# One decoder step with a 32-expert layer: products that nobody reads ahead of the first gather, the first extra job written out, and the memory key weights in two loads

## What is computed

```python
def memory_kv(mem, g_mem_kv, w_mk, w_mv):          # 256 memory tokens
    m = rmsnorm(mem, g_mem_kv)
    k = (m @ w_mk).reshape(b, n, MEM_HEADS, MEM_HD)
    v = (m @ w_mv).reshape(b, n, MEM_HEADS, MEM_HD)

def moe_ffn(h, ...):                                # 32 experts, 4 for each token
    logits = (xt @ w_router) + b_router
    top_val, top_idx = lax.top_k(logits, TOP_K)
    gates = jax.nn.softmax(top_val, axis=-1)
    ...
        g = jnp.minimum(xblk @ w_gate[e] + b_gate[e], 7.0)
        u = jnp.clip(xblk @ w_up[e] + b_up[e], -7.0, 7.0)
        a = (u + 1.0) * (g * jax.nn.sigmoid(1.702 * g))
        return a @ w_down[e] + b_down[e]            # times the gate, added to the token

y_prompt, y_sample = rmsnorm(x, g_final)
```

## Time and profile before

| what | value |
|---|---|
| median of 3 runs | 1349.05 us (1343.01 to 1349.41) |
| the profiled execution, its own time | 1347.15 us |
| its span in the trace | 1345.3 us |
| TensorE busy | 1291.2 us (96%) |
| VectorE busy | 450.1 us (33%) |
| moved by DMA | 463.37 MB, 344 GB/s over the span |
| mean granted clock | 0.982 |

### The profile page before, as it was taken

One profiled execution on the slowest core, in us unless ns is written; L12 is line 12 of the kernel. 1 busy time (PEld: TensorE's weight loads), 2 busy tenths in 40 slices (PEclk: granted clock), 3 DMA queues, 4 the chain that ended last, 5 costly groups with the idle time before them and its releaser, 6 DMA issues.

```text
span 1345.3 us, 15553 instructions
## 1 busy us (share of the span) xinstructions
PE 1291.2 (96%) x6088; PEld 523.6 (39%) x6088; DVE 450.1 (33%) x1124; ACT 217.1 (16%) x442; POOL 15.5 (1%) x20
## 2 busy tenths in 40 slices
PE   7999898999799999999999999999999999999996
PEld 3665654556433333333333333333333333333332
DVE  1168778334532222322223322223222222222233
ACT  3014433314311010101001011101111101010102
POOL 0100020000000000000000000000000000000000
PEclk9999899999789999999999999999999999999998
DMA  9701132490879999999999999999999999999993
GB/s 343 280 12 42 36 111 94 169 393 1 340 307 411 426 428 427 428 429 428 429 427 427 428 427 428 428 428 429 427 428 428 427 428 428 428 429 427 427 427 120
DMA packets 44265, 463.37 MB, mean 344 GB/s; under 512 B 5206, under 2 KB 6166, under 8 KB 17860
## 3 DMA queue, kind: packets, MB, share of 16 engines
q1 hardware_dynamic: 42700, 453.54, 80.6%
q0 software_dynamic: 1536, 9.44, 1.9%
HBM read 460.04 MB, written 3.28 MB: 344 GB/s over the span
## 4 chain that ended last, share of the span: by engine, by line
PE 79%; DMA 14%; DVE 5%; ACT 1%; issue 1%; SPq 0%; ACTq 0%; DVEq 0%
PE psum L891 42%; DMA ring<-in_w_up 13%; PE psum L866 6%; PE psum L324 6%; PE psum L907 4%; PE psum L403 3%; PE psum L884 2%; PE psum L363 2%; PE psum L619 2%; DVE ring L1543 1%; PE psum L742 1%; PE psum L381 1%; PE psum L911 1%; PE psum L590 1%; PE psum L748 1%; DMA ring<-in_w_mk 1%
## 5 line engine op out<-in xcount | busy, mean ns | idle before, releaser
L891 PE MATMUL psum<-ring,work 128*64 128x512 f32 x3168 | 702.1, 597 | 7.3 <-DMA ring<-in_w_up 7.3
L891 PEld LDWEIGHTS psum<-ring,work 128*64 128x64 f32 x3168 | 221.5, 137 | 478.2 <-issue 446.6
L1927 DVE TENSOR_SCALAR work<-psum 128x512 f32<-128x512 f32 x32 | 22.1, 692 | 378.9 <-PE psum L891 378.9
L866 PE MATMUL psum<-H,work 128*64 128x512 f32 (+1 forms) x408 | 101.0, 614 | 1.4 <-DVE work L1818 1.4
L1936 DVE TENSOR_SCALAR work<-psum 128x512 f32<-128x512 f32 x32 | 22.1, 692 | 170.1 <-PE psum L891 170.1
L1891 DVE TENSOR_TENSOR X<-X,psum 128x512 f32<-128x512 f32 x68 | 46.7, 686 | 90.0 <-PE psum L907 89.9
L1543 DVE SCALAR_TENSOR_TENSOR ring<-ring,cwT 128x256 f32<-128x256 f32 x240 | 72.5, 377 | 0.1
L1408 ACT COPY work<-psum 128x512 f32<-128x512 f32 x32 | 18.7, 586 | 292.7 <-PE psum L866 292.7
L1415 ACT COPY work<-psum 64x512 f32<-64x512 f32 x32 | 18.5, 578 | 286.6 <-PE psum L891 286.6
L324 PE MATMUL psum<-C,work 128*128 128x128 f32 (+5 forms) x371 | 57.1, 288 | 6.6 <-DMA work<-in_small_rows 6.4
L324 PEld LDWEIGHTS psum<-C,work 128*128 128x128 f32 (+5 forms) x371 | 49.0, 187 | 31.1 <-issue 22.4
(11 more groups left out here) (291 smaller groups left out, 913.3 us busy)
## 6 DMA issues: line engine op xcount, KB each, us to landing
ring<-in_w_gate SPq DMA_DIRECT2D x66, 2048.0 KB, 24.3
ring<-in_w_up SPq DMA_DIRECT2D x66, 2048.0 KB, 25.9
ring<-in_w_down SPq DMA_DIRECT2D x66, 2048.0 KB, 27.9
ring<-in_w_in SPq DMA_DIRECT2D x1, 4096.0 KB, 27.3
ring<-in_cache_mem_k SPq DMA_DIRECT2D x8, 512.0 KB, 14.8
ring<-in_cache_mem_v SPq DMA_DIRECT2D x8, 512.0 KB, 16.3
ring<-in_w_in SPq DMA_DIRECT2D x1, 2688.0 KB, 22.3
ring<-in_w_mk SPq DMA_DIRECT2D x1, 2048.0 KB, 10.3
```

The costliest lines, as they stand in the source:

```text
L866: last = mm(psum[64 * nh:64 * nh + 64, 2, :], Ph[0:ROWS[tt], tt, :], xn[0:ROWS[tt], tt, 512 * nh:512 * nh + 512], start=tt == 0, stop=tt == 2)
L891: last = mm(psum[64 * nh:64 * nh + 64, bank, :], src[:, j, 64 * half:64 * half + 64], w[:, half, j, 512 * nh:512 * nh + 512], start=first ...
```

## The change

1. Start: `small_rows` is issued ahead of `mem`, and `wmk` comes in two loads of 1 MB with a semaphore each. PE does inner blocks 0 to 3 for both memory tiles, then 4 to 7.
2. Router: `keep_warm` issues products of the identity with itself into a PSUM bank that nobody reads, 10 ahead of the wait for `routed`, 5 ahead of the wait for `p_built`.
3. The first extra job is no longer the first round of a loop but written out for all engines, and done whether there is one or not (where there is none, its ranks are moved away by 1000, so that nothing is selected). Its gate and up products stand between the five pieces of the last pair. The gather of a job to come is gone; a loop for jobs 2 and on gathers for itself at its beginning.
4. ACT squares and takes the root of each tile as soon as its x is final (`ov_scm`), into ring slot 3, not after all three.

```diff
+            emptied(pe, V, ("mT", 1, 1))
+            pe.wait_ge(s.load_wmk, 16)
+            keys = [A.open(pe, ("mk", tt)) for tt in range(2)]
+            for k0 in (0, 4):
+                if k0:
+                    pe.wait_ge(s.load_wmk2, 16)
+                for tt in range(2):
+                    for k in range(k0, k0 + 4):
+                        last = mm(keys[tt], mT[:, k, 128 * tt:128 * tt + 128], wmk[:, k, :], start=k == 0, stop=k == KD - 1)
+                    if k0:
+                        last.then_inc(s.full_a, 1)
...
+            def keep_warm(n):
+                for _ in range(n):
+                    mm(psum[:, 1, 0:128], ident, ident, start=True, stop=True)
+            keep_warm(10)
             pe.wait_ge(s.routed, 1)
...
             last.then_inc(s.rank_full, 1)
+            keep_warm(5)
...
+            pe.wait_ge(s.ov_xtm, 1)
+            pe.wait_ge(s.ov_p, 1)
+            biases(0)
+            for half in range(2):
+                pe.wait_ge(ring_in[0][half], (1 + USES) * 16)
+                product(0, XT[0], 0, half, False, half == 1).then_inc(ring_used[0][half], 1)
+            turn_gates(s.ov_pt)
             pe.wait_ge(s.y_moved, NE + 1)
             pe.wait_ge(s.pgt_moved, NE // 2 + 1)
-            for piece in range(5):
-                scatter_pair(piece, NE // 2 + 1, 5 * (NE // 2))
+            scatter_pair(0, *last_pair)
+            scatter_pair(1, *last_pair)
+            for half in range(2):
+                pe.wait_ge(ring_in[1][half], (1 + USES) * 16)
+                product(1, XT[0], 1, half, False, half == 1).then_inc(ring_used[1][half], 1)
+            scatter_pair(2, *last_pair)
+            scatter_pair(3, *last_pair)
+            pe.wait_ge(s.ov_a, 1)
+            turn(4, AA, s.ov_at)
+            scatter_pair(4, *last_pair)
+            pe.wait_ge(s.ov_atm, 1)
+            for half in range(2):
+                pe.wait_ge(ring_in[2][half], (1 + USES) * 16)
+                product(2, AT, 2, half, half == 0, half == 1).then_inc(ring_used[2][half], 1)
+            pe.wait_ge(s.ov_ym, 1)
+            pe.wait_ge(s.ov_ptm, 1)
+            pe.wait_ge(s.sc_free, 5 * (NE // 2) + 7)
+            for tt, bank in enumerate(OV_BANKS):
+                for nh in range(2):
+                    last = scatter_one(tt, nh, 0, bank)
+                last.then_inc(s.ov_sc, 1)
...
-                    pe.wait_ge(s.ov_p, n + 1)
-                    gather(s.ov_xg)
...
             dma(C[:, 0:128], a["constants"][:, 0:128]).then_inc(s.load_ident, 16)
+            dma(small_rows, a["small_rows"]).then_inc(s.load_ident, 16)
             dma(mem, a["mem_prompt"][0].rearrange("(t p) d -> p t d", p=P)).then_inc(s.load_mem, 16)
-            dma(small_rows, a["small_rows"]).then_inc(s.load_ident, 16)
-            dma(wmk, rows_of(a["w_mk"][0])).then_inc(s.load_wmk, 16)
+            dma(wmk[:, 0:4, :], rows_of(a["w_mk"][0])[:, 0:4, :]).then_inc(s.load_wmk, 16)
+            dma(wmk[:, 4:8, :], rows_of(a["w_mk"][0])[:, 4:8, :]).then_inc(s.load_wmk2, 16)
...
+            job = sp.value_load(jobs[0:1, 1:2], min_val=0, max_val=NE - 1)
+            for kind in range(3):
+                src = weights(kind, job)
+                for half in range(2):
+                    sp.wait_ge(ring_used[kind][half], USES)
+                    load_half(kind, half, src)
...
+            f(small[:, 17:18], eps[:, :], ACT.Sqrt)
+            for tt in range(3):
+                act.wait_ge(s.ov_scm, tt + 1)
+                last_root(tt)
...
+            gate_of(1)
+            dve.wait_ge(s.sc_free, last_pair[1] + 2)
+            add_scattered(0, *last_pair)
+            add_scattered(1, *last_pair)
+            up_of(1)
+            add_scattered(2, *last_pair)
+            turned_of(1)
+            add_scattered(3, *last_pair)
+            add_scattered(4, *last_pair)
+            dve.wait_ge(s.sc_free, last_pair[1] + 7)
+            further = dve.value_load(jobs[0:1, 0:1], min_val=0, max_val=JOBS)
+            add_of(1)
```

More of the change, by code:

```diff
@@ L121 @@
+            self.place_full, self.spread_ready, self.lists_full, self.ov_rank, self.load_ident, self.load_lat,
+            self.qz_ready, self.load_wmk2, self.load_wout2, self.load_wout3, self.full_s, self.free_s, self.part_full,
+            self.part_moved, self.gates_ready, self.gt_full,
+        ) = [new(f"signal{i}") for i in range(109)]
 class Lane:
@@ L1418, in _, with last_root @@
             further = act.value_load(jobs[0:1, 0:1], min_val=0, max_val=JOBS)
-            with act.If(further > 0):
-                with act.Fori(1, further + 1) as n:
+            act.wait_ge(s.ov_gc, 1)
+            f(sgm, gm, ACT.Sigmoid, scale=ALPHA).then_inc(s.ov_sg, 1)
+            act.wait_ge(s.ov_pt, 1)
+            nc.scalar.copy(PgT[0], psum[:, 5, 0:T]).then_inc(s.ov_ptm, 1)
+            act.wait_ge(ring_used[2][1], 1 + USES)
+            nc.scalar.copy(Y[0][0], psum[:, 2, :]).then_inc(s.ov_ym, 1)
+            def last_root(tt):
+                r = ROWS[tt]
+                n = st(f(squares[0:r, tt, :], X[0:r, tt, :], ACT.Square, accum_out=small[0:r, 8 + tt:9 + tt]))
+                st.wait(n)
+                f(small[0:r, 11 + tt:12 + tt], small[0:r, 8 + tt:9 + tt], ACT.Sqrt, bias=eps[0:r, :],
+                  scale=1.0 / D).then_inc(s.x_root, 1)
+            f(small[:, 17:18], eps[:, :], ACT.Sqrt)
+            for tt in range(3):
+                act.wait_ge(s.ov_scm, tt + 1)
+                last_root(tt)
+            with act.If(further > 1):
+                with act.Fori(2, further + 1) as n:
+                    act.wait_ge(s.ov_xg, n - 1)
+                    nc.scalar.copy(XG, psum[:, 2, :]).then_inc(s.ov_xgm, 1)
                     act.wait_ge(s.ov_gc, n)
@@ L1424, in _ @@
                     nc.scalar.copy(PgT[0], psum[:, 5, 0:T]).then_inc(s.ov_ptm, 1)
-                    act.wait_ge(s.ov_xg, n)
-                    nc.scalar.copy(XG, psum[:, 2, :]).then_inc(s.ov_xgm, 1)
                     act.wait_ge(ring_used[2][1], n + USES)
                     nc.scalar.copy(Y[0][0], psum[:, 2, :]).then_inc(s.ov_ym, 1)
-            f(small[:, 17:18], eps[:, :], ACT.Sqrt)
-            act.wait_ge(s.x_done, 1)
-            for tt in range(3):
-                r = ROWS[tt]
-                n = st(f(xn[0:r, tt, :], X[0:r, tt, :], ACT.Square, accum_out=small[0:r, 8 + tt:9 + tt]))
-                st.wait(n)
-                f(small[0:r, 11 + tt:12 + tt], small[0:r, 8 + tt:9 + tt], ACT.Sqrt, bias=eps[0:r, :],
-                  scale=1.0 / D).then_inc(s.x_root, 1)
+                act.wait_ge(s.x_done, 1)
+                for tt in range(3):
+                    last_root(tt)
         @block.vector
@@ L1910, in _ @@
             first = dve.value_load(jobs[0:1, 1:2], min_val=0, max_val=NE - 1)
+            base = lists[:, NE + 1:NE + 2]
+            st(v.tensor_scalar(place[:, 2:3], base, 0.0, -1000.0, ALU.is_equal, ALU.mult))
+            st.wait()
             for tt in range(3):
                 r = ROWS[tt]
[L1913 to L1914 removed]
+                v.tensor_scalar(routing[0:r, tt, 2, NE:NE + 1], routing[0:r, tt, 2, bass.ds(first, 1)], base[0:r],
+                                place[0:r, 2:3], ALU.subtract, ALU.subtract)
                 v.tensor_copy(routing[0:r, tt, 1, NE:NE + 1], routing[0:r, tt, 1, bass.ds(first, 1)])
@@ L1952, in _ @@
             dve.sem_inc(s.ov_xtm, 1)
-            last = 5 * (NE // 2)
-            dve.wait_ge(s.sc_free, last + 2)
-            for piece in range(5):
-                add_scattered(piece, NE // 2 + 1, last)
-            dve.wait_ge(s.sc_free, last + 7)
-            further = dve.value_load(jobs[0:1, 0:1], min_val=0, max_val=JOBS)
-            with dve.If(further > 0):
-                with dve.Fori(1, further + 1) as n:
-                    take_job(n + 1)
-                    dve.wait_ge(ring_used[0][1], n + USES)
-                    v.tensor_scalar(gm, psum[:, 0, :], LIMIT, None, ALU.min).then_inc(s.ov_gc, 1)
-                    dve.wait_ge(s.ov_rank, n + 1)
-                    dve.wait_ge(s.ov_pt, n)
+            last_pair = NE // 2 + 1, 5 * (NE // 2)
```

115 lines of the change are left out of this document (61 added, 54 removed).

## The result

The changed kernel takes 1331.47 us (median of 4 runs, 1329.55 to 1332.83) against 1346.24 us for the kernel before on the same chip (median of 4, 1343.01 to 1349.41). The ratio is 0.9889, interval 0.9856 to 0.9923: 1.1% faster. The forecast was 1331, with 1325 to 1341 as its range. The profiled execution took 1331.66 us; its span is 1329.5 us and its mean granted clock 0.992.

The account below looks back on a forecast made before the run. The prediction took the stream of expert weights, full from the third refill on, to bound the kernel. Start 1.9, router 7.6, extra job 5.1 and final norm 1.8 sum to 16.4 us: 1347.15 to 1330.8, said as 1331, range 1325 to 1341.

Parts of the forecast that it names:

- What bounds the kernel: Expert stage: the weight stream runs without stop from the third refill, so a microsecond earlier at expert 0's gate counts fully.
- the ceiling that the forecast worked out: Router: the gain cannot exceed the hole in the weight stream by much; at most 8.2 us.
- Start, 1.9 us: Key products: `mT` rather than 2 MB of key weights ends the wait, at 10.6 instead of 12.54; gain 1.9 us.
- Router, 7.6 us: Logits to expert 0's gate product: unread products bring the clock back before the gather; gain 7.6 us.
- gather 2.72 instead of 5.61 [...] gate 9.69 to 7.02: Router: gather and expert 0's gate product at full clock, worth 3.15 and 2.67 us.
- The price of 0.5 us for an unread product: Router: a 128x128 product costs 0.5 us at 1.2 GHz and 0.25 at 2.4 GHz, read from L859.
- Extra job, 5.1 us: Expert 31's end to the job's down product: 33.7 us shrink to 28.6 without useless gather, turnings and waits; gain 5.1 us.
- without that cover 2.3 us would be open: Extra job: pieces 2 to 4 cover DVE's two operations up to `AA` (1.6 us) and the `AT` copy (0.7 us).
- Final norm, 1.8 us: End of kernel: ACT's squares start after the first addition, DVE's scalings follow its additions; gain 1.8 us, 1.0 to 2.2.
- The clock that doesn't come back: Rival at the router: clock still low before the gather, which runs at 1.2 GHz; 1340 (to 1342) us; chance 0.13.
- The clock that falls again: Rival between gather and first gate product: clock returns, then falls; some 3.5 of 7.6 us missing, 1334.5 us; chance 0.15.
- The slower case: Rival: useless products in the way, clock at 1.2 GHz far into the expert loop; 1356 us with one expert; chance 0.03.

Follow-up runs that it names:

- e_piecesfirst_fill: Changed kernel with the last pair's five pieces ahead of all the job's products, plus six unread products behind the up product; 1336.69 us, ratio 0.9937.
- e_same: The kernel before, unchanged, run again; 1344.58 us (median of 12), ratio 0.9998.
- e_warm: The kernel before with only the 10 and 5 unread products added; 1341.30 us (median of 12), ratio 0.997.
- e_nowarm: The changed kernel without its 15 unread products; 1336.17 us (6 runs), ratio 0.9926.
- e_rootlate: The changed kernel with ACT's squares and roots begun only after DVE's third addition; 1335.28 us (6 runs), ratio 0.9929.
- e_piecesfirst: Changed kernel with the last pair's five pieces put back ahead of the job's products; useless gather and loop stay out; 1336.45 us, ratio 0.9938.
- e_nostart: The changed kernel with the old order of loads and old loop of key products; 1333.12 us (6 runs), ratio 0.9918.
- e_warm10_0: The changed kernel with the first 10 unread products but without the 5 ahead of the gather; 1335.48 us (5 runs), ratio 0.9914.
- e_fill: The changed kernel with 4, 2 and 1 more unread products in the waits ahead of the router's logits; 1331.37 us (5 runs), ratio 0.9907.

## Why the prediction was right

The time was hit (1331 for 1331.47), and of each of the four parts some gain is there in the profiles. The sizes of the terms came out less well, and part of the hit is luck, as shown below. By term, against the pair of profiles:

*What bounds the kernel.* Right. Behind the third refill the stream is full from about 398 on (thirteenth slice, 428), ends 9.7 us earlier, and the end moved with it and with the tail. Of the 9.4 us by which the third refill was issued earlier, 8.4 arrived at the last wait for weights. What became of the other 1.0 us isn't shown. It needn't be the ceiling that the forecast worked out: in e_piecesfirst_fill the gate product ends 1.7 us earlier still (374.71) and the landing comes 2.4 us earlier (1269.61), with nothing lost.

*Start, 1.9 us.* Half of it. `mT` does end the wait, but the key products begin at 11.58, not at 10.6: `mem` landed at 7.07 and its turning could not begin earlier, so all of it hangs on a transfer that I had moved by 0.3 us only. They end 0.8 us earlier in this pair. Over four profiles with the old start and nine with the new one the ends are 1.7 us apart in the mean, but they overlap (40.28 to 44.05 and 38.72 to 41.81), and the times say 1.1, within their noise. (The forecast put 0.43 us against 29.43 / 64, which is 0.46; it bears on nothing.)

*Router, 7.6 us.* Right for the execution it was read from, too large for the kernel. Logits to gate product shrank from 27.9 to 20.1 us, 7.8, as the sum had it: ten products in 3.94 us (forecast below 4.4), gather 2.97, gate 7.02, clock back at about 360, where about 361.7 was forecast. But the same program has 22.1 us in e_same, and the two comparisons by time give 3 to 4 us (e_warm) and 2.2 to 4.1 (e_nowarm). The step that was mis-sized is "gather 2.72 instead of 5.61 [...] gate 9.69 to 7.02": it took the low clock until 381 as a property of the kernel, where it is one of several courses. The total was hit all the same because the sum was made against that very execution, whose 1347.15 us lie 2 us above the median of all 45 runs of before beside the experiments (1345.2), and whose low clock stood in both the base and the term. Nor do start and router together (0.8 + 7.8) make up the 9.4 us by which the gate product ends earlier: the logits are 1.6 us earlier, twice what the start gave at 41 us, and the runs don't say why. That these 0.8 us and the 0.8 by which the extra job gave more make up for the 1.1 that the start lacked is luck. (The price of 0.5 us for an unread product was read from L859, whose products are 128x32 and not 128x128; it was right all the same, 4.43 us for ten at 1.2 GHz in e_rootlate.)

*Extra job, 5.1 us.* Right in size (5.9), and half wrong in reason. The size holds beyond the pair: from the landing to the end of the down product it is 50.0 us in all three profiles with the old tail and 44.1 in all nine with the new one. The forecast put 2.72 us of it down to the gather "for a job that does not exist" and 0.75 to its turnings. e_piecesfirst leaves both out and gains nothing (50.0 us), and with the clock held 1.4 us (48.6). They had covered two waits for DVE. The forecast named these waits ("without that cover 2.3 us would be open"; 1.59 and 0.78 are 2.4) and that pieces 2 to 4 cover them now, so its sum was sound, yet which edit earns the gain was not. It is the order, with 4.5 of the 5.9 us.

*Final norm, 1.8 us.* 1.5: the roots gave 1.2 of it. DVE's three scalings follow its additions (to 1321.48) as forecast, with some 0.4 us between. By the times, e_warm and e_nostart differ in the tail and the roots alone, and are 8.2 us apart by the medians and 7.0 by the ratios, where the profiles say 5.9 + 1.5 = 7.4.

*Rivals.* The clock that doesn't come back wasn't seen: nine profiles here have all fifteen products, the gather takes 2.97 us in each of them (4.34 to 5.61 in the five without or with part of them), and logits to gate product 19.4 to 20.6. The clock that falls again is real, and is what the one profile without the five shows (e_warm10_0). The rule of the Trainium skill (TensorE: Matmul & The Clock Gate, Part 4: PE-mode transpose), that turning doesn't count as busy in the same way, is neither borne out nor refuted: in e_fill the clock stayed at 1.00 across turnings with other products between them, and no run here had turnings alone. The second fall in e_warm10_0 came among turnings, small products and waits, which doesn't separate them either. The slower case had nothing for it.

*The typical gain.* Against 1345.2 the changed kernel's 1332 are 13.2 us: some 3.5 from the products, 5.9 from the extra job, 1.5 from the norm and 1.1 to 1.7 from the start, 12.0 to 12.6. The rest, 1 us, is within what these medians tell.

## What to carry to other kernels

Before an instruction without a reader is counted as a gain, look what wait it stands in: taken out alone, the gather and its turnings were worth nothing in one profile and 1.4 of their 3.5 us in the other, and moving real work into that wait and the one for ACT's copy was worth 4.5 to 5.9 us. A term that hangs on the granted clock is read from more than one execution of the kernel before, since the clock's course differs between them; sum and base at least come from the same one. And where cheap products fill one wait, look at the next one too: ten without the five bought, in the one profile taken, a clock that fell again before the gather. Last, a stretch that comes out the same in every profile (50.0 against 44.1 us here) can be trusted where the whole time moves by several us from one execution to the next.

## What the runs showed of the hardware

Unchanged code ranged over 11 us (1339.71 to 1350.87) with the mean granted clock between 0.989 and 0.983. Where the clock falls and how long it stays isn't fixed by the program: from 354.2 to about 381 in one execution of before, from 360.6 to about 371 in another (e_same).

Behind 7 us of dense products, a wait of 1.59 us, four turnings (0.75 us) and a wait of 0.78 us, the clock fell at the end of the second wait (e_piecesfirst, at about 1312.8; 0.50 between 1314 and 1316), while the same spot with six unread products in the first wait held 1.00 (e_piecesfirst_fill).

At the start, the recorded clock and the pace disagree. The window of the changed kernel (columns as above) says 1.00, where the kernel before has 0.50 between 14 and 16 and 0.93 between 16 and 18:

```profile
12.00:14.00 2.00, 2.00 (x3) 0.75 (x3) 0.17 (x1) 0.24 (x1) 0.00 (x0) 1.00 1.02 406
```

The weight loads of the key products in the same profile (timeline of PEld):

```profile
13.44 0.34 PEld L365 LDWEIGHTS psum<-ring 128*128 128x128 f32 x1 [0.52 <-issue]
14.30 0.34 PEld L365 LDWEIGHTS psum<-ring 128*128 128x128 f32 x1 [0.52 <-issue]
15.15 0.31 PEld L365 LDWEIGHTS psum<-ring 128*128 128x128 f32 x1 [0.52 <-issue]
15.70 0.19 PEld L365 LDWEIGHTS psum<-ring 128*128 128x128 f32 x1 [0.24 <-issue]
16.13 0.19 PEld L365 LDWEIGHTS psum<-ring 128*128 128x128 f32 x1 [0.24 <-issue]
```

They stand 0.86 us apart until 15.15 and 0.43 from 15.70 on: half speed and full speed, whatever the clock's row says. For the first 15 us of this kernel the pace is the better witness. The Trainium skill (TensorE: Matmul & The Clock Gate, Part 1) warns that the recorded clock events have been unreliable; this start agrees. At the router row and pace went together: 9.53 to 9.69 us for a gate product begun at 0.50, 7.02 at 1.00.
